# Moving the sample attention of a two-layer decoder step one projection step ahead, with spare TensorE products at the waits

## The reference

```
gq, gk, gv, gg, glr, mu, mv, sq, sk, sv = split_cols(a @ w_in)
o_gla, s_gla = gla_mixer(...)          # gated linear attention, 4 heads
o_gm, v_gm = gmlp_mixer(mu, mv, ...)   # spatial gating, 4 heads
# stick-breaking attention, 8 heads; samples: 1024 paged keys and the new ones
z = einsum(q, k) * HEAD_DIM ** -0.5 + bias
log1m = where(mask, -softplus(z), 0);  suffix = reversed cumsum(log1m) - log1m
A = where(mask, exp(log_sigmoid(z) + suffix), 0);  o = A @ v
out = concat([o_gla, o_gm, o_sb]) @ w_out
```

## Time and profile before

| | us |
|---|---|
| median of 3 runs | 1377.99 |
| range of the runs | 1376.77 to 1379.05 |
| profiled execution, its own time | 1375.78 |
| its span, first to last instruction | 1374.0 |
| TensorE busy in it | 1319.2 (96%) |
| VectorE, ScalarE, GpSimd busy | 794.7, 585.5, 81.8 |
| mean granted TensorE clock | 0.989 |

### The profile page before, as it was taken

The page is one execution under the profiler, slowest core; times in us unless marked ns, Lnnn a source line. Parts: engine busy times, 40 slices in busy tenths (PEclk is TensorE's granted clock), DMA queues, the critical chain, the costliest instruction groups (busy, mean ns, idle before and its releaser), DMA issues.

```text
span 1374.0 us, 34334 instructions
## 1 busy us (share of the span) xinstructions
PE 1319.2 (96%) x13994; PEld 1261.2 (92%) x13994; DVE 794.7 (58%) x1160; ACT 585.5 (43%) x963; POOL 81.8 (6%) x158
## 2 busy tenths in 40 slices
PE   6899999999989899999999999999999998999998
PEld 4899999998977899999989999998997797999998
DVE  2555553568885555555465555446788657555544
ACT  2533333443565443334453333445346546333343
POOL 4000000010041000000000000002003100000000
PEclk9899999999999999999999999999999998999999
DMA  9978789789998895568875666996998993565453
GB/s 328 269 230 257 217 251 313 218 256 339 302 304 292 274 322 154 153 174 274 266 237 154 170 167 204 294 268 202 333 337 266 329 301 100 160 174 155 137 168 98
DMA packets 424009, 324.59 MB, mean 236 GB/s; under 512 B 15656, under 2 KB 351912, under 8 KB 423889
## 3 DMA queue, kind: packets, MB, share of 16 engines
q1 hardware_dynamic: 421124, 317.03, 76.2%
q0 software_dynamic: 2464, 5.71, 1.3%
q10 hardware_dynamic: 300, 0.13, 0.0%
HBM read 318.03 MB, written 4.78 MB: 235 GB/s over the span
## 4 chain that ended last, share of the span: by engine, by line
PE 81%; DVE 6%; DMA 5%; SPq 3%; ACT 3%; issue 1%; DVEq 1%; POOL 0%; ACTq 0%
PE PS L626 22%; PE PS L627 22%; PE PS L628 22%; PE PS L652 3%; DMA raw<-in_ffn_w_in 2%; SPq L454 2%; PE PS L680 1%; PE PS L910 1%; PE PS L681 1%; PE PS L682 1%; DVE w_lo L1718 1%; DMA raw<-in_mix_w_in 1%; SPq L493 1%; DVE direct L1994 1%; PE PS L965 1%
## 5 line engine op out<-in xcount | busy, mean ns | idle before, releaser
L1718 DVE TENSOR_TENSOR w_lo<-raw,w_hi 128x1024 fp32r<-128x1024 f32 (+1 forms) x368 | 392.8, 1106 | 450.1 <-ACT w_hi L1332 449.6
L1332 ACT ACTIVATE w_hi<-raw 128x1024 fp32r<-128x1024 f32 (+1 forms) x368 | 338.0, 960 | 658.9 <-PE PS L628 574.3
L626 PE MATMUL PS<-a_hi,w_hi 128*128 128x288 f32 x1760 | 523.9, 298 | 0.0
L627 PE MATMUL PS<-a_lo,w_hi 128*128 128x288 f32 x1760 | 519.2, 295 | 0.0
L628 PE MATMUL PS<-a_hi,w_lo 128*128 128x288 f32 x1760 | 517.7, 294 | 0.3 <-issue 0.3
L626 PEld LDWEIGHTS PS<-a_hi,w_hi 128*128 128x128 f32 x1760 | 329.8, 187 | 3.9 <-issue 3.5
L628 PEld LDWEIGHTS PS<-a_hi,w_lo 128*128 128x128 f32 x1760 | 331.4, 188 | 0.6 <-issue 0.6
L627 PEld LDWEIGHTS PS<-a_lo,w_hi 128*128 128x128 f32 x1760 | 330.4, 188 | 0.3
L627 PE MATMUL PS<-h_lo,w_hi 128*128 128x288 f32 x704 | 208.4, 296 | 0.0
L626 PE MATMUL PS<-h_hi,w_hi 128*128 128x288 f32 x704 | 208.1, 296 | 0.0
L628 PE MATMUL PS<-h_hi,w_lo 128*128 128x288 f32 x704 | 208.0, 296 | 0.0
(11 more groups left out here) (323 smaller groups left out, 1136.1 us busy)
## 6 DMA issues: line engine op xcount, KB each, us to landing
raw<-in_ffn_w_in SPq DMA_DIRECT2D x176, 512.0 KB, 5.0
direct<-in_cond_w SPq DMA_DIRECT2D x240, 256.0 KB, 4.9
direct<-in_cache_sb_k SPq DMA_DIRECT2D x128, 256.0 KB, 4.5
direct<-in_cache_sb_v SPq DMA_DIRECT2D x104, 256.0 KB, 4.4
raw<-in_ffn_w_out SPq DMA_DIRECT2D x64, 384.0 KB, 3.8
raw<-in_mix_w_in SPq DMA_DIRECT2D x48, 512.0 KB, 7.2
raw<-in_ffn_w_out SPq DMA_DIRECT2D x64, 320.0 KB, 4.4
side<-in_cond_w SPq DMA_DIRECT2D x48, 256.0 KB, 5.2
```

What stands on the lines that cost most here:

```text
L626: pe.matmul(out, whi, hi, start=begins and i == 0, stop=False)
L627: pe.matmul(out, whi, lo, start=False, stop=False)
L1332: act.activation(w_hi[:, s, at_:at_ + n], raw[:, s, at_:at_ + n], ACT.Copy)\
L1718: tt(w_lo[:, s, at_:at_ + n], raw[:, s, at_:at_ + n], w_hi[:, s, at_:at_ + n], ALU.subtract).then_inc(lo_done.sem, 1)
```

## The change

- Keys: the key chunks and their transposes stand one step earlier (steps 2 to 9), and so do their loads in SP's order; the queries are spread and transposed after the first half of step 2; `modulation` goes from step 1 to step 3.
- Scores, sample sums 0, totals, offsets 0 and weights 0 go from the last steps and the attention stage into steps 4 to 11, the first regrouping to the end of step 11, into banks 4 to 7. The cap of the second half goes from GpSimd to VectorE, sample sums 1 stand behind the gate's sums, ahead of the prompt scores.
- The three key rows are transposed in steps 10 and 11.
- The attention stage has a new order on TensorE, VectorE and ScalarE: value chunks start between the prompt scores, and values_by_sample goes behind the second weights_by_page.
- The first regrouping reads a tile of its own, `a_turn0`, that lies over `extra`; so the load of value chunk 4 waits for it, and the first two output weights are issued ahead of it.
- `spare_products`: products of the identity with itself into unused columns, at the start and around the seams. Nothing reads them. 1 and 3 of them also stand in each of `mixer_seam` and `layer_seam`, ahead of the first pair of squares and ahead of `spread_x`.
- In the seam of layer 1 after the mixer, three conditioning chunks go from behind the root to ahead of the squares.

The diff, cut to its core:

```diff
-    KEYS_AT = {j: (2 * j - 6, 2 * j - 5) for j in range(3, 11)}
+    KEYS_AT = {j: (2 * j - 4, 2 * j - 3) for j in range(2, 10)}
...
+        a_turn0 = tile("a_turn0", [P, 4 * NPG * 32], F32, at[0] - 8192)
...
-                    sp.wait_ge(direct_used.sem, direct_used.at(l, DP_K + NPC))
+                    sp.wait_ge(a_moved.sem, a_moved.at(l, 1))
...
-                mix_in(2, 3)
+                mix_in(2)
                 key_chunks(l, 0, 1)
+                mix_in(3)
+                key_chunks(l, 2, 3)
                 mix_in(4)
-                key_chunks(l, 2, 3)
-                mix_in(5)
                 for j in range(3, 9):
-                    mix_in(j + 3)
-                    key_chunks(l, *(n + 4 for n in KEYS_AT[j]))
+                    mix_in(j + 2)
+                    key_chunks(l, 2 * j - 2, 2 * j - 1)
+                mix_in(11)
                 for n in range(NPC):
                     if n % 5 == 4:
                         extra_chunk(l, n)
                     else:
                         page_chunk(l, cache_sb_v, DP_V, 4 * n, n - (n + 1) // 5)
-                    if n == 4:
+                    if n == 3:
...
+            def spare_products(n, bank):
+
+                for _ in range(n):
+                    pe.matmul(PS[:, bank, 3 * P:4 * P], ident[:, :], ident[:, :], start=True, stop=True)
...
                 for j in range(KP):
+                    spare_products((1, 3, 1, 1)[j], 5)
                     pair_squares(l, seam, j)
+                spare_products(3, 5)
                 spread_x(*divmod(3 * l + seam + 1, 3))
                 for n in range(middle, end):
                     cond_chunk(layer, x, dp, *divmod(n, 4))
+                if middle == end:
+                    spare_products(9, 1)
...
+                spare_products((0, 0, 1, 5)[s], 3)
                 cond_chunk(None, 0, 0, 1, s)
+            spare_products(12, 3)
...
+                            if (j, h) == (2, 0):
+                                pe.wait_ge(cond_copied.sem, cond_copied.at(l, 12))
+                                pe.wait_ge(q_rep.sem, q_rep.at(l, 1))
+                                for p in range(PR):
+                                    turned = pe.transpose(PS[:, 6, p * P:p * P + P],
+                                                          qrep[:, p, :, :].rearrange("d a s -> d (a s)"), ident[:, :])
+                                turned.then_inc(q_t.sem, 1)
+                            if (j, h) == (10, 0):
+                                pe.wait_ge(gate_x.sem, gate_x.at(l, 1))
+                                part_offsets(0, 7)
+                            if (j, h) == (11, 0):
+                                pe.wait_ge(z_got.sem, z_got.at(l, 5))
+                                rows_of(2, SK, 5, k_t)
...
+                    if j == 10:
+                        rows_of(0, SK, 6, k_t)
+                        pe.wait_ge(z_got.sem, z_got.at(l, 4))
+                        rows_of(1, SK, 4, k_t)
+                    if j == 11:
+                        pe.wait_ge(off_added.sem, off_added.at(l, 1))
+                        pe.wait_ge(kv_k.sem, kv_k.at(l, 3))
+                        regroup(0)
...
-                part_offsets(0, 7)
+                pe.wait_ge(mix_evac.sem, mix_evac.at(l, N_MI + 2))
+                prompt_scores(0)
...
+                value_chunk(0)
+                prompt_scores(2)
...
+                pe.wait_ge(c_sub.sem, c_sub.at(l, 1))
                 regroup(1)
                 new_values(0)
-                pe.wait_ge(kv_v.sem, kv_v.at(l, 2))
-                rows_of(1, SV, 5, v_t)
+                pe.wait_ge(a_copied.sem, a_copied.at(l, 2))
+                prompt_sums(1, 2)
+                value_chunk(8)
...
+                spare_products(5, 4)
...
-                filled_seam(l, 1, 2, DP_C[0], 0, 4 if l + 1 < L else 1, 7 if l + 1 < L else 4, l)
+                filled_seam(l, 1, 2, DP_C[0], 0, 4, 7 if l + 1 < L else 4, l)
...
+                        scores(3)
+                        sample_weights(0)
                     if j == 11:
-                        act.preload_act_table_set(SILU_TABLES)
-                        act.activation(Fm[:, GG:GG + 2, :], Fm[:, GG:GG + 2, :], ACT.Silu)
-                        act.preload_act_table_set(LOG_TABLES)
-                        scores(3)
+                        key_rows(0, 6)
+                        key_rows(1, 4)
+                        sample_log1p_exp(1)
+                        key_rows(2, 5)
...
+                weights_by_page(0)
...
                 prompt_scores(2)
                 prompt_scores(3)
-                sample_log1p_exp(1)
+                prompt_log1p_exp(0)
                 gla_rows(0, 6)
-                weights_by_page(0)
-                key_rows(2, 4)
-                prompt_log1p_exp(0)
+                prompt_log1p_exp(1)
                 gla_rows(2, 6)
+                sample_weights(1)
                 value_rows(2, 1)
-                prompt_log1p_exp(1)
-                values_by_sample()
-                sample_weights(1)
                 value_rows(0, 2)
-                prompt_log1p_exp(2)
+                value_rows(1, 3)
                 weights_by_page(1)
                 sample_rows(0)
-                value_rows(1, 3)
+                prompt_log1p_exp(2)
+                act.wait_ge(gvk_a.sem, gvk_a.at(l, 2))
+                values_by_sample()
...
+                    if j == 8:
+                        sample_sums(0)
...
-                        sample_sums(0)
+                        sample_offsets(0, 7)
+                        sample_cap(1)
+                    if j == 11:
+                        turn_weights(0)
...
+                sample_sums(1)
```

More of the change, by code:

```diff
@@ L985, in turn_rows, with rows_of @@
                     last.then_inc(o_turned.sem, 1)
+                def rows_of(i, f0, bank, done):
+                    sl, n = token_tile(i)
+                    for p in range(PR):
+                        last = pe.transpose(PS[0:n, bank, p * P:p * P + P], Fm[:, f0 + p, sl], ident[:, :])
+                    last.then_inc(done.sem, 1)
                 for j in range(N_MI):
@@ L1082, in prompt_values @@
                     last.then_inc(op_sum.sem, 1)
-                def rows_of(i, f0, bank, done):
-                    sl, n = token_tile(i)
-                    for p in range(PR):
-                        last = pe.transpose(PS[0:n, bank, p * P:p * P + P], Fm[:, f0 + p, sl], ident[:, :])
-                    last.then_inc(done.sem, 1)
                 def gla_rows(i, bank):
@@ L1501, in weights_by_page, with key_rows @@
                     for p in range(PR):
+                        bank = p if g else 4 + p
                         out = a_keys[:, :, 32 * p:32 * p + 32].rearrange("k n (s e) -> k s n e", s=4)
-                        last = act.activation(out, PS[:, p, 0:256].rearrange("k (s n e) -> k s n e", s=4, e=8), ACT.Copy)
+                        last = act.activation(out, PS[:, bank, 0:256].rearrange("k (s n e) -> k s n e", s=4, e=8), ACT.Copy)
                     last.then_inc(a_copied.sem, 1)
+                def key_rows(i, bank):
+                    n = P if i < PT_ else NS
+                    act.wait_ge(k_t.sem, k_t.at(l, i + 1))
+                    act.activation(kst[0:n, i, :], PS[0:n, bank, :], ACT.Copy).then_inc(kv_k.sem, 1)
                 for j in range(N_MI):
@@ L1513, in _ @@
                         split(l, POS_MI, j // 2 + 1, j % 2)
+                    if j == 4:
+                        scores(0)
                     if j == 5:
@@ L1531, in _ @@
                         sample_log1p_exp(0)
+                        scores(2)
                     if j == 9:
@@ L2055, in _ @@
                         sample_queries(0)
-                    for n in KEYS_AT.get(j, ()):
-                        if n:
-                            turn_keys(n)
+                        sample_queries(1)
                     if j + 2 < N_MI:
                         split(l, POS_MI, j // 2 + 1, j % 2)
-                    if 3 <= j < 10:
-                        sample_queries(j - 2)
+                    if j == 2:
+                        turn_keys(2)
+                        turn_keys(3)
+                    if j == 3:
+                        own = lambda a, k: vec[:, a:a + k]
+                        modulation(2, (1, own), own)
+                    if 3 <= j < 9:
+                        sample_queries(j - 1)
                     if j == 4:
```

120 lines of the change are left out of this document (48 added, 72 removed).

## The result

The changed kernel takes 1389.54 us (median of 5, 1384.68 to 1392.75), the kernel before beside it 1376.77 us: a ratio of 1.0095, 95% interval 1.0073 to 1.0116. It is slower, and lies 5.5 us above the range of the prediction. The profiled execution is the slowest of its five, 1392.75 us with a span of 1391.0, so its trace shows 3 us more than is typical.

The account below looks back on a forecast made before the run. TensorE, 96% busy, was taken as the bound, so only its standing time and half clock could be won. From 1375.8 us, minus 3.9 for spares, plus 6.5 for mixers, gave 1378.4, forecast as 1378 us; range 1370 to 1384.

Parts of the forecast that it names:

- Spare products: Start and seams after the mixers: full clock, with the moved last-seam chunks, wins 3.9 us (1 to 5.6).
- the seam gains of 1.0 and 1.9 us: Seams after the mixers: layer 0 gains 1.0 us (0 to 1.7), layer 1 gains 1.9 us (1.3 to 2.4).
- Projection steps: Twelve projection steps with keys one step sooner: +0.2 us per layer, about 0.5 us of gaps recoverable in layer 1.
- wait for the transposed queries: Projection step 2: TensorE waits 1.0 us for the queries' copy, held up on VectorE by step 3's remainders.
- Attention stage: Attention stages: new waits sum to 8.6 us for 5.3 and 4.9 before; +3.3 us in layer 0.
- on zp: Attention stage: TensorE waits 1.8 us for a prompt-score bank, as sample sums 1 precede all prompt scores on VectorE.
- gla_rows(2): Attention stage: TensorE waits 1.7 us before this row product, through the same lateness.
- the second softplus: Attention stage: TensorE waits 1.35 us before the third sums, since VectorE needs 3.95 us between sums against 2.6.
- the last one: Attention stage's end: TensorE waits 3.0 us for the last softplus, with values_by_sample now behind the second regrouping.
- New half clock: Attention stages: the 3.0 us wait can lower the clock again, charged 1.5 us for both layers (0 to 3.4).
- Rival 2: Projection steps 3 to 8: key transposes on VectorE become the pace, 0.5 us per step, +6, 1384 us; chance 0.18.
- Rival 3: Clock not held: the 3.9 us gain halves and the layers pay 3.4 instead of 1.5; 1382 us, chance 0.10.

Follow-up runs that it names:

- e1: The kernel before with all 67 spare products and the moved conditioning chunks of the last seam, nothing else; ratio to the kernel before 1.0012.
- e15: The kernel before with spare products, moved last-seam chunks and 32 tiny products at the very start (half a packet's shift); ratio to the kernel before 1.0010.
- e2: The changed kernel without its spare products, the moved chunks of the last seam kept; ratio to the kernel before 1.0078.
- e16: The changed kernel without its spare products and with 32 tiny products at the start (half a packet's shift); ratio to the kernel before 1.0096.
- e9: The changed kernel with 32 tiny products at the very start, shifting later instructions by half a packet; 1380.14 us, ratio to the kernel before 1.0032.
- e17: The changed kernel with 96 tiny products at the start, a shift of one and a half packets; 1380.49 us, ratio to the kernel before 1.0044.
- e6: The changed kernel with values_by_sample back ahead of the second weights_by_page, between the value rows; ratio to the kernel before 1.0064.
- e13: The changed kernel with 32 tiny products at the start and values_by_sample back ahead of the second weights_by_page; ratio to the kernel before 1.0017.
- e5: The changed kernel with 64 tiny products in the seam ahead of each mixer, a whole packet more each; ratio to the kernel before 1.0208.
- e12: The changed kernel with 24 products adding zero in each attention stage, ahead of five TensorE waits; ratio to the kernel before 1.0050.
- e14: e13 with 16 products adding zero in each attention stage, ahead of four TensorE waits; ratio to the kernel before 1.0028.

## Why the prediction was wrong

The forecast was 1378, no change; the measured time is 11.5 us more.

- **Spare products, -3.9 us: wrong.** They take 0.22 us each, as forecast, and the half clock in the seams went. But e1 and e15 measure +0.1% where -0.3% was forecast. The step that failed is the price: the seam gains of 1.0 and 1.9 us were taken as kept, and the spares were charged under 0.1 us per seam. The half clock itself is there in all six traces without spares (3.4 to 6.8 us of it in the seam after mixer 0, 10.2 to 13.7 us in the last) and gone in nearly all with them. Yet over 19 of the traces (13 with spares, 6 without; the stages scatter by 1 us, so this is rough) the start is 0.5 us shorter with spares, the seam after mixer 0 0.3 us, the last seam with the rest 1.0 us, which is 1.8 us where 3.9 was forecast; and the two seams ahead of the mixers are 0.6 and 0.7 us longer. If the +0.1% holds in the new order too, this is 5 us of the miss; there e2 and e16 leave it open. Whether more of the 3.9 would show with the packets well placed, no run says.
- **Projection steps, +0.2 a layer: wrong by its omissions.** The wait for the transposed queries came as forecast (1.1 us between products in both layers, forecast 1.0), the wait for the transposed keys went, none for late transposes appeared. What was missed is no wait for another engine: the stand of 1.7 and 2.2 us at an instruction packet, and the half clock behind the second. No term of the sum stood for it. Shifting the packets (e9, e17) takes 8.7 and 7.0 us off the time. Even then the stage is 1.0 and 0.8 us longer, which is no new cost: 1.7 us of products, the key rows and the first totals, now start here and not in the attention stage, and the forecast moved them in neither row. The mixer as a whole is the fair comparison: +3.3 and +2.9 us in e9, where +3.5 and +1.5 were forecast, with 1.5 for half clock in both.
- **Attention stage: right in mechanism, high by 1 us in layer 0.** Each named wait is there: on zp 1.5 (forecast 1.8), gla_rows(2) 1.6 (1.7), the second softplus about 1.2 (1.35), the last one 1.6 and 3.0 (3.0). The stage came to +2.5 in layer 0 and, in e9, to +2.3 and +2.1, where +3.3 and +2.0 were forecast. Two reasons can be read: the products that moved out of the stage, and a slip in the sum, where 21.5 + 0.8 + 0.6 is 22.9 and not 23.2, so that the wait on zp should have been forecast as 1.5, which is what it was. That the 3.0 comes from values_by_sample is shown by e6, and by e13 against e9: TensorE's waits for the softplus in layer 0 fall from 4.1 to 1.7 us.
- **New half clock, +1.5 us: mis-sized in this execution.** There were 6.8 us at half in the attention stage of layer 0, mostly absorbed by the wait behind it, and 3.4 and 13.7 us in that of layer 1, the latter worth 6.8 us. It followed the 3.2 us that TensorE stood before the last suffix sums. e17's profiled execution has the same in layer 0 (below), and both executions are the longest of their kernels, while e9 with the same wait of 3.2 us in layer 0 ran on at full clock. In all 20 traces there are eight such waits of 2.9 us or more ahead of the last suffix sums; three are followed by 13.7 us at half clock (the changed kernel, e17, e5), five are not. So it comes in some executions only, and explains part of the 3 us between the profile and the median. Half clock ahead of such a wait can cost little: e9 has 10.2 us of it from 1081.9, ahead of the last suffix sums of layer 1, where the last wait is then 1.5 us in place of 2.9. What it costs in a typical execution is open: e12 says up to 6 us, e14 none.
- **Rivals.** Rival 2 named nearly the price of the projection steps (+6), but its mechanism, VectorE as the pace, isn't in the trace: no product waits for a transposed key. Rival 3 (clock not held, 1382) is partly what happened, in the mixers and not in the seams. Nothing in the list was a cost of TensorE's own instructions, and that step was missing, though TensorE's waits in the trace of before list five stands of the conditioning products, 4.5 us in all, ended by "issue", and the three longest of them end 1.3 to 1.5 us after an instruction packet had landed.

The window of e17 behind its last suffix sums of layer 0 (columns as above):

```profile
430.00:446.00 16.00, 13.58 (x100) 8.10 (x102) 3.49 (x6) 4.78 (x6) 0.00 (x0) 0.57 0.33 114
```

With the packets at the good place the trace of e9 sums to +2.7 us over the profile of before, where the forecast had +2.6. Part of that agreement is luck: the medians say +4.4 us, and the spares gave nothing that could be measured in the old order.

Open: why a packet's request comes up to 1.6 us sooner or later in the same code, and what the half clock costs in the median.

## What to carry to other kernels

When an edit adds or removes instructions on TensorE, time it at two or three places of the instruction packets (some hidden tiny products at the start) before the edit is judged; where the order is dense in small matmuls under full DMA load, this alone was worth 0.6%. In an attention-like stage of long chains, look for work off the chain (values_by_sample) that stands behind the last rendezvous, and move it into the idle stretch before. Spare products raise the granted clock; whether they raise the speed has to be measured, for what is won in a seam can be lost in the next stage, and the added instructions move the packets.

## What was not expected of the hardware

- Where the 16 KB packet of its instructions started between 0.7 us before and 0.2 us after the beginning of a run of 64 matmuls of 4 columns that follows 64 of 128, TensorE stood 1.3 to 2.2 us in 11 of 12 cases; from 0.8 us on, no stand was seen in 26.
- In all twelve cases TensorE went on 1.3 to 1.7 us after the packet had landed, and the packet itself took 1.0 to 1.2 us.
- One fp32 product of 128x128 is two matmuls and two weight loads in the trace: 67 spare products are 134 matmuls, and 32 products shift the code by half a packet.
- A tiny product costs by where it goes: 64 matmuls in four column groups side by side started within 0.57 us, 119 in one column group (e5) within 3.8 us.
